# RWKV scan: the transposed factor of a triangular inverse carried by products in place of whole transposes

## The reference

```python
def wkv7_scan(r, w, k, v, a, b, reverse):
    def step(S, inp):
        rt, wt, kt, vt, at, bt = inp
        sa = jnp.einsum('bhvk,bhk->bhv', S, at)
        S = S * wt[:, :, None, :] + sa[..., None] * bt[:, :, None, :] + vt[..., None] * kt[:, :, None, :]
        return S, jnp.einsum('bhvk,bhk->bhv', S, rt)
    _, y = lax.scan(step, jnp.zeros((Bn, H, N, N), jnp.float32), xs, reverse=reverse)
    return jnp.moveaxis(y, 0, 1)
```

## Time and profile before

| | |
|---|---|
| median of 3 runs | 1836.87 us (1836.57 to 1841.27) |
| the profiled execution, span from first to last instruction | 1827.0 us |
| PE busy | 1665.2 us, 91% of the span |
| DVE / ACT / POOL busy | 62% / 46% / 15% |
| granted clock of PE, mean over the span | 0.976 |
| the same in the 14 scan steps read below | 1.00 |

### The profile page before, as it was taken

How to read it: one execution, slowest core, us unless ns; L and a number is a source line. 1 busy time by engine, 2 the same in 40 slices (tenths; PEclk the granted TensorE clock), 3 DMA queues, 4 the chain that set the end, 5 groups by cost and what they waited for, 6 DMA issues and landing times. The chain is left out here.

```text
span 1827.0 us, 41748 instructions
## 1 busy us (share of the span) xinstructions
PE 1665.2 (91%) x17234; PEld 1262.1 (69%) x17234; DVE 1136.0 (62%) x1971; ACT 843.7 (46%) x1342; POOL 267.6 (15%) x337
## 2 busy tenths in 40 slices
PE   5999999998988898888987995999999999999995
PEld 4667777786765787777876884766666666666662
DVE  5558888845676544565556674666566556656754
ACT  4346656422222444444443112655565566556533
POOL 0020000002120543443440000100000000000003
PEclk9999999999999999999998995999999999999997
DMA  5224454524134222222213247699899899989927
GB/s 170 81 93 112 133 145 119 150 78 176 70 111 173 61 62 62 62 61 60 63 49 114 70 150 276 272 374 373 341 372 374 363 365 368 380 342 371 389 105 288
DMA packets 100357, 355.24 MB, mean 194 GB/s; under 512 B 16776, under 2 KB 56072, under 8 KB 85737
## 3 DMA queue, kind: packets, MB, share of 16 engines
q1 hardware_dynamic: 87528, 306.83, 45.5%
q0 software_dynamic: 8064, 29.36, 4.1%
q10 hardware_dynamic: 4608, 16.78, 2.2%
HBM read 294.75 MB, written 56.10 MB: 192 GB/s over the span
## 5 line engine op out<-in xcount | busy, mean ns | idle before, releaser
L2380 DVE TENSOR_TENSOR e_rl<-proj,e_rh 128x1024 fp32r<-128x1024 f32 x256 | 304.6, 1222 | 145.3 <-ACT e_rh L2316 144.3
L2316 ACT ACTIVATE e_rh<-proj 128x1024 fp32r<-128x1024 f32 x256 | 258.8, 1054 | 49.6 <-PE e_ph L51 30.3
L51 PE MATMUL e_ph<-e_rh,e_xh 128*128 128x512 f32 x512 | 220.9, 431 | 16.5 <-DVE e_rl L2380 13.9
L2297 PE MATMUL e_py<-mix,proj 128*128 128x512 f32 x512 | 225.0, 592 | 0.7 <-issue 0.7
L51 PE MATMUL e_ph<-e_rh,e_xl 128*128 128x512 f32 x512 | 201.6, 394 | 0.0
L51 PE MATMUL e_ph<-e_rl,e_xh 128*128 128x512 f32 x512 | 200.9, 392 | 0.0
L51 PE MATMUL a_b<-a_xh,a_wh 128*128 128x512 f32 x432 | 177.7, 411 | 5.7 <-DVE a_wl L587 3.2
L2297 PEld LDWEIGHTS e_py<-mix,proj 128*128 128x128 f32 x512 | 97.0, 190 | 110.8 <-issue 108.1
L51 PE MATMUL a_b<-a_xh,a_wl 128*128 128x512 f32 x432 | 169.7, 393 | 0.0
L51 PE MATMUL a_b<-a_xl,a_wh 128*128 128x512 f32 x432 | 169.6, 393 | 0.0
L51 PEld LDWEIGHTS e_ph<-e_rh,e_xh 128*128 128x128 f32 x512 | 97.4, 190 | 47.3 <-DVE e_rl L2380 19.6
(11 more groups left out here) (383 smaller groups left out, 3191.9 us busy)
## 6 DMA issues: line engine op xcount, KB each, us to landing
proj<-in_moe_w SPq DMA_DIRECT2D x64, 2048.0 KB, 14.3
mix<-in_moe_w SPq DMA_DIRECT2D x32, 2048.0 KB, 8.6
proj<-scan_operands SPq DMA_DIRECT2D x64, 320.0 KB, 3.5
expert_rows<-e_yo ACTq DMA_DIRECT2D x32, 512.0 KB, 11.2
scan_operands<-late SPq DMA_DIRECT2D x56, 256.0 KB, 2.6
proj<-in_w_in SPq DMA_DIRECT2D x27, 512.0 KB, 4.1
proj<-in_x SPq DMA_DIRECT2D x16, 512.0 KB, 6.5
expert_rows<-proj SPq DMA_DIRECT2D x1, 7680.0 KB
```

Of the source, the lines that this page charges most:

```text
L51: m = e.matmul(out, lhs[a], rhs[b], start=first and n == 0, stop=last and n == 2)
L2297: m = e.matmul(py[h][:, :], at[:, k, :], w2[j][:, k, h * HALF:(h + 1) * HALF], start=(k == 0), stop=(k == KF - 1))
L2316: e.activation(rh[s % RING][:, :], piece(j, s), ACT.Copy).then_inc(high, 1)
L2380: e.tensor_tensor(rl[s % RING][:, :], piece(j, s), rh[s % RING][:, :].bitcast(F32), ALU.subtract).then_inc(low, 1)
```

## The change

Both forms, T and H, are now made by products. `ts` and a new PSUM region `us` lie side by side (`both`); behind the T product stands a second one, U, with the two operands exchanged, which gives the next H; one ACT copy of 512 columns takes T and H to the new tile `s_th`, in place of `s_tt` and `s_hu`. The 16 transposes a step and ACT's eight copies of `s_hu` are gone; at level 5 only one product is made. At level 1, U writes banks that the T product of the other half also writes, so PE waits for its own T products (`t_done`); at the other levels the order of the halves changes from level to level (`half_and_other`) so that this isn't needed. The copy to `s_hf` moves from DVE to ACT. POOL writes the first mask for each g by itself, right behind that g's `s_h1`.

The list `fill` is replaced by `inside(l)` (between X and T) and `between(l)` (behind T and U), with another distribution: `a_k_v` now belongs to the step itself and stands inside level 1; `outputs_by_v` and `outputs_by_u` stand inside level 2; `chunk_sums` and `states` 0 behind level 2; `states` 1 inside level 3, ahead of `products`; `outputs_by_state` behind level 3. DVE's copy of the maps comes at level 2 instead of 1.

```diff
-        tt, xx = sb("s_tt", [P, GP, HU, CH]), sb("s_xx", [P, GP, 2, 2, CH])
-        hu = sb("s_hu", [P, GP, 2, 2 * CH])
+        th, xx = sb("s_th", [P, GP, 2, 2, 2, CH]), sb("s_xx", [P, GP, 2, 2, CH])
...
-        hus = [t[:, 0, 4 * CH:8 * CH].rearrange("p (q c) -> p q c", q=2) for t in lv]
+        us = [t[:, :, 4 * CH:6 * CH].rearrange("p b (q c) -> p b q c", q=2) for t in lv]
+        both = [t[:, :, 2 * CH:6 * CH] for t in lv]
...
+                def level_one_applied(n):
+                    for g in range(GP):
+                        e.wait_ge(x_kept, n * 10 + (g + 1))
+                        for q, p, c in cells("qpc"):
+                            i = mm(ts[g][hs[c], p, q, :], h1[hs[c], g * HU + 2 * q + p, :], xx[hs[c], g, p, q, :], start=True, stop=True)
+                        i.then_inc(t_done, 1)
+                    for g in range(GP):
+                        e.wait_ge(t_done, n * 2 + (g + 1))
+                        for q, p, c in cells("qpc"):
+                            i = mm(us[g][hs[p], c, q, :], xx[hs[c], g, p, q, :], h1[hs[c], g * HU + 2 * q + p, :], start=True, stop=True)
+                        i.then_inc(th_full, 1)
...
+                def level_applied(n, l):
+                    for g in range(GP):
+                        e.wait_ge(x_kept, n * 10 + (2 * (l - 1) + g + 1))
...
+                        for q, p, c in cells("qpc" if l % 2 == 0 else "pqc"):
+                            r, o, h, x = factors(q, p, c)
+                            lhs, rhs = (x, h) if l == LEVELS - 1 else (h, x)
+                            i = mm(ts[g][hs[c], r, o, :], lhs, rhs, start=True, stop=True)
+                        if l < LEVELS - 1:
+                            for q, p, c in cells("cqp"):
+                                r, o, h, x = factors(q, p, c)
+                                i = mm(us[g][hs[o], r, c, :], x, h, start=True, stop=True)
+                        i.then_inc(th_full, 1)
...
-                        if not first:
-                            for g in range(GP):
-                                for q in range(2):
-                                    i = e.transpose(hus[g][:, q, :], tt[:, g, 2 * q:2 * q + 2, :].rearrange("p u c -> p (u c)"),
-                                                    S.ident[:, :])
-                                i.then_inc(x_full, 1)
...
-                        if l > 1:
-                            for g in range(GP):
-                                e.wait_ge(x_kept, n * 10 + (2 * (l - 1) + g + 1))
-                                e.activation(hu[:, g, :, :], hus[g], ACT.Copy).then_inc(hu_kept, 1)
...
-                                e.activation(tt[:, g, :, :].rearrange("p (q b) c -> p b q c", b=2), ts[g][:, :, :, :], ACT.Copy
+                                e.activation(th[:, g, :, :, :, :].rearrange("p b k q c -> p b (k q c)"), both[g], ACT.Copy
                                              ).then_inc(th_kept, 1)
...
+                        e.tensor_tensor(al[:, 0, g * HU:(g + 1) * HU, :], ab, bcast(level[:, 1, :], HU), ALU.mult
+                                        ).then_inc(al_ready, 1)
```

More of the change, by code:

```diff
@@ L1 @@
+import itertools
 import math
@@ new lines, in step, with inside, between @@
+                def step(n, back, front):
+                    def inside(l):
+                        if l == 1:
+                            if back is not None:
+                                inverse_applied(back)
+                            a_k_v(n)
+                        if l == 2 and back is not None:
+                            outputs_by_v(back)
+                            outputs_by_u(back)
+                        if l == 3:
+                            if back is not None:
+                                states(back, 1)
+                            if front is not None:
+                                products(front, 0, back)
+                        if l == 4 and front is not None:
+                            products(front, 1, back)
+                        if l == 5 and front is not None:
+                            turn(front, 1, back)
+                    def between(l):
+                        if l == 1 and back is not None:
+                            chunk_maps(back)
+                        if l == 2 and back is not None:
+                            chunk_sums(back)
+                            states(back, 0)
+                        if l == 3 and back is not None:
+                            outputs_by_state(back)
+                        if l == 4 and front is not None:
+                            turn(front, 0, back)
+                    level_one(n)
+                    inside(1)
+                    level_one_applied(n)
+                    between(1)
+                    for l in range(2, LEVELS):
+                        level(n, l)
+                        inside(l)
+                        level_applied(n, l)
+                        between(l)
@@ L1555, in first @@
                     turn(f, 1, None)
-                    a_k_v(f)
                 def last(m):
@@ L1617, in step @@
                         if l == 2 and back is not None:
-                            states(back, 0)
+                            maps(back)
                         if l == 2 and unit_of(n) is not None:
                             unit_centre(e, y, stat, unit_of(n), u_centred)
+                        if l == 2 and back is not None:
+                            states(back, 0)
+                        if l == 3 and back is not None:
+                            states(back, 1)
                         if l == 3 and front is not None:
                             products(front, 0)
-                        if l == 3 and back is not None:
-                            states(back, 1)
                         if l == 4 and front is not None:
```

91 lines of the change are left out of this document (34 added, 57 removed).

## The result

The changed kernel takes **1878.65 us** (median of 4 runs, 1876.34 to 1882.93) against 1839.07 us for the kernel before in the same comparison (1836.57 to 1842.28): ratio 1.0226, 95% interval 1.0206 to 1.0247. By the ratio that is +41.5 us; the two medians differ by 39.6. It is slower, as forecast, but by about twice the forecast's +21.5, and just above the upper end of the range, 1878.

The account below looks back on a forecast made before the run. Instruction fetch was taken as the bound under PE: 688 matmuls at 28.7 ns (19.75 us), tail 4.95 and 0.15 made 24.85 against 23.3 us a step; +22.5 over 15 steps, step 0 giving back 1, gave 1858 us, range 1843 to 1878.

Parts of the forecast that it names:

- fast part: Scan step outside the tail: 688 matmuls forecast, nearly all bound by instruction fetch, 19.75 us a step.
- Fetch is not hidden: Denies the rival that fetch is hidden: "issue" idles have another cause, only PE's own sum counts; 1836 us, chance 0.14.
- the middle of 27.0 and 30.4: Forecast price per fast-part matmul, 28.7 ns, between the fetch floor and the old step's mean.
- PE's own clock: PE's work and waits without fetch: new step 19.95 us against 20.0, from -0.6 to +0.6 us a step.
- the one for `s_hf`: Step's end: X(1) directly follows T(5) and waits for ACT's hf copy, about 0.45 us.
- the one ahead of the second turn: Second turn comes before DVE's copy of the first is kept, a wait of about 0.2 us.
- The tail now has 144: Level 4's T and U through level 5: 144 matmuls in 4.95 us, 34 ns each, slower than fetch.
- the +1.5: Forecast growth of a scan step, 24.85 us against 23.3.
- Step 0 gives back 1 at most: First scan step: at most 1 us taken off the +22.5 us of the 15 steps that have neighbours.
- some 10 us lie outside the span: Whole execution: median 1836.9 us against a span of 1827.0; the change does not touch the difference.
- The chain was the bound: Rival for the scan: no new wait is real and stalls do not grow; -9 us, 1828 us, chance 0.14.
- Fetches collide with the operand loads: Rival for the fast part: half the pages pay 34 ns a matmul; +3.5 us a step, 1889 us, chance 0.10.

Follow-up runs that it names:

- bare products: Kernel before with independent, wait-free 64x64 float32 products behind the scan (64, 16, 128 columns, then 64 beside operand loads); run once, 2075.89 us with the added work.
- by blocks: Kernel before with X and T of level 1 as block-diagonal 128x128 products, 16 matmuls each in place of 32; 1864.38 us, ratio 1.0161.

## Why the prediction was right in direction and too small

**Right: the bound.** PE is held by the arrival of its instructions, in pages of 128 matmuls. The bare products show it without any of the kernel's dependences, and it follows the count: fewer matmuls by 96 gave 2.83 us a step, by 32 gave 0.87, and the fast part took 28.7 to 28.8 ns a matmul with 656, 720 and 752 of them. Fetch is not hidden, so that rival falls, and with it, for PE in this kernel, the Trainium skill's rule that it is mostly hidden ("Runtime: NRT & Kernel Launch", section "Instruction fetch mechanics"). The same section's block of 256 instructions agrees with the 128 matmuls and 128 loads between two stalls.

**Right: the price.** 28.7 ns was taken for a matmul of the fast part, and after shows 28.7: 752 in 21.56 us. The kernels without transposes there lie at 27.8 to 28.8, those with them at 30.0 to 31.1 (34.0 by blocks, where the array is the bound). That the middle of 27.0 and 30.4 hit so well is in part luck: no row showed it, its reason was only argued, and without the operand loads the same kernel pays 27.8.

**Right: PE's own clock.** Its busy time grew by 1.9 us in 14 steps. Of the new waits two show, the one for `s_hf` with 0.34 us where 0.45 was forecast and the one ahead of the second turn with 0.16 where 0.2 was; the others don't show in the list. One that does, for DVE's `s_xx` (3.2 us in four idles), was not in the forecast. The quiet tail behind the turn takes 3.96 us, where the prediction's terms for it (4.95 and 0.15, less 1.1 for T and U of level 4) give 4.00.

**Wrong: where the fast part ends.** The step that failed is "The tail now has 144 (T and U of level 4, both turns, X and T of level 5) in 4.95 us, 34 ns each, still slower than the fetch." The mean of 34 ns hides two things: 64 matmuls at 17 ns, then 80 at 48. Slow transposes behind the 64 can't shorten a stall that falls among them, and in every second step one does. So they belong to the fast part: 64 x 28.7 = 1.84 us and not 1.1, +0.74 a step; read from the trace, they took 1.86. The turn and what follows came to 4.32 on the mean and not 4.00, +0.32; 0.18 of that are three waits for DVE's `s_xx` at level 5 (2.5 us in all), which the sum did not have. Together 24.85 + 0.74 + 0.32 = 25.91, measured 25.88. Over 15 steps these two terms are 16 of the 20 us that were missing. The rest is about what step 0 has, below.

**Right, but not told apart: the dealing.** The new dealing, `a_k_v` above all, cost 8.3 us by the medians (4 to 13) and 0.62 us a step by the traces, without any product added. It was in the sum, among the 688 matmuls at the fetch's price; the prediction never named it as a part of the +1.5. The other 33 or so of the 41.5 us came with the exchange of the transposes for the second product.

**Wrong: step 0 and the start and end of the execution.** "Step 0 gives back 1 at most": it took 20.27 us against 16.42 of before (this is the window from its X product to the next):

```profile
601.81:618.23 16.42, 14.69 (x473) 1.00 0.29 83
...
591.20:597.90 6.70, 4.07 (x78) 0.50 0.02 4
```

Two things are in it. One is the granted clock: at 0.50, the lower level of 1.2 GHz, for 17.0 us in after, 4.4 of them in step 0, and for 6.7 us, ahead of step 0, in before. In after PE had no matmul in the 2.1 us from 590.0 before it fell. That is not the change's: before without loads has a step 0 of 17.87 us at 0.87, so the clock is worth about 1.5 us. The other is the count: step 0 has 577 matmuls where before had 473, since U is made there too, which the sum had left out; that is the other 2.4 us. And PE stood for 3.84 us ahead of a page at 1007.50, near the scan's end, with 225 GB/s of loads for the next stage under way. Such events were not in the sum. Nor do "some 10 us lie outside the span": in after and in the experiments the time is 2 to 3 us above the span (1879.71 against 1877.6). The profiled execution of before was a quick one: 1827.0 and 2 to 3 us make 1829 to 1830, some 9 us below the median of 1839.07, and single executions of before do go down to 1828.22. Of the difference of the two spans, 50.6 us, that much is chance. It lies in these places: 2.9 us ahead of step 0, 3.9 in step 0, 36.2 in the 14 steps, 7.7 behind them. How the chance is spread over them is not known. Some of it may be in the 14 steps: without loads before gained 8.5 us by the medians but 2.0 in the 14 steps of the traces. So the 23.3 us a step that the prediction built on may be some tenths low.

**The rivals.** "The chain was the bound" needed a page under 2.8 us; no page of the bare products took less than 3.47 us. "Fetches collide with the operand loads" came near in its total (1889), but for the wrong reason: without loads the distance between the kernels is 36.5 of 41.5 us, and no step of after pays the 34 ns a matmul that it had read in a bad step.

What stays open: whether an added X product really costs 36 ns a matmul, why the kernels with transposes pay 30 to 31 ns in the fast part, and how the chance of the profile of before is spread.

## What to carry to other kernels

In code of many small matmuls count instructions as well as array time: cut the trace where an idle ends for which nothing was waited, count what lies between two such ends, and if it is always the same number, that idle is the fetch. A slow stretch pays only for what is fetched during it, so set the boundary between what pays the fetch and what doesn't in front of the slow instructions, not by a mean over a group that holds both. (The one attempt here to gain time by this, the transposes spread among products, gained nothing.) Replacing one slow instruction by several fast ones then costs by their number, and moving fast work out of a slow stretch costs too.

## What the runs showed of the hardware

- The time of a page comes in steps: in the sections with 64 columns, by the starts in the timeline, 3.48 or 3.75 us without loads (once 4.03) and mostly 3.75 or 4.03 beside loads of 90 GB/s, so 0.27 us or twice that above the shortest, and nothing between.
- At the lower level of the clock a page took at most 0.2 us more, though the array itself nearly filled it: at a granted clock of 0.50, with 16 columns, five pages took 3.81 us each; at 1.00, with 64 columns, 3.59.
- Equal pages, one after another, each had their stall of 1.4 to 1.9 us. After the end of the scan, where PE had waited for other engines, 194 bare matmuls ran without one (986.10), the last 66 of a page and a whole page more, and then PE stood for 3.30 us. So one page was in hand, and no more; the prediction's "a slow page banks nothing for the next" is not quite so.
- A float32 product of 64 columns on the whole array with a weight load of 128 columns took 120 ns a record (1.92 us for 16), one on a quarter some 26 ns at level 1 and 16 ns among many. (All at a granted clock of 1.00.)
- The granted clock fell to 0.50 at the scan's start in both kernels, for 6.7 and for 17.0 us.
